# A gated delta rule stage with its units reordered, small transposes and sums taken off the matrix engine, and its steps placed anew

## What is computed

```python
qkv = causal_conv_silu(concat([d_q, d_k, d_v]), conv_w)
q = l2norm(q) * DN_HEAD_DIM ** -0.5 ; k = l2norm(k)
g = -exp(dn_a_log) * softplus(d_a + dn_dt_bias) ; beta = sigmoid(d_b)
# per chunk of C tokens, per head
decay = exp(where(tri, g_cum_i - g_cum_j, -inf))
a = where(strict, (k * beta) @ k.T * decay, 0)
T = inverse(a + eye)                         # unit lower triangular
value = T @ (v * beta) ; k_cumdecay = T @ (k * beta * exp(g_cum))
attn_intra = where(tri, q @ k.T * decay, 0)
# over the chunks, with the state S
v_new = value - k_cumdecay @ S
o = (q * exp(g_cum)) @ S + attn_intra @ v_new
S = S * exp(g_last) + (k * exp(g_last - g_cum)).T @ v_new
out_b = rmsnorm(o) * silu(d_z)
```

## Time and profile before

| | us |
|---|---|
| median of 3 runs (lowest, highest) | 2085.27 (2084.6, 2088.63) |
| the profiled execution | 2087.39 |
| its span, first to last instruction | 2085.8 |
| PE busy | 2041.2 (98%) |
| DVE busy | 1043.2 (50%) |
| ACT busy | 840.2 (40%) |
| POOL busy | 140.3 (7%) |

### The profile page before, as it was taken

One profiled execution on the slowest core, in us unless ns is written; L12 is line 12 of the kernel. 1 busy time (PEld: TensorE's weight loads), 2 busy tenths in 40 slices (PEclk: granted clock), 3 DMA queues, 4 the chain that ended last, 5 costly groups with the idle time before them and its releaser, 6 DMA issues.

```text
span 2085.8 us, 28890 instructions
## 1 busy us (share of the span) xinstructions
PE 2041.2 (98%) x9864; PEld 1677.5 (80%) x9864; DVE 1043.2 (50%) x1773; ACT 840.2 (40%) x1612; POOL 140.3 (7%) x162
## 2 busy tenths in 40 slices
PE   7999999999999999999999999999999999998999
PEld 6788778887888888878878888888888888887887
DVE  5644564656566555464454444454444444445332
ACT  6643344443443434443344434343343444344221
POOL 1000010211121111001100000000000000000110
PEclk9999999999999999999999999999999999999999
DMA  9422111111111121224432222222212222222432
GB/s 369 185 101 80 61 62 60 66 55 59 62 60 60 40 80 61 91 96 137 150 131 87 78 88 85 80 85 80 105 73 94 80 85 80 94 73 100 151 134 77
DMA packets 31858, 198.10 MB, mean 95 GB/s; under 512 B 4016, under 2 KB 4144, under 8 KB 11088
## 3 DMA queue, kind: packets, MB, share of 16 engines
q1 hardware_dynamic: 23040, 164.64, 22.0%
q0 software_dynamic: 8064, 30.81, 4.1%
q10 hardware_dynamic: 720, 2.19, 0.3%
HBM read 189.23 MB, written 8.39 MB: 95 GB/s over the span
## 4 chain that ended last, share of the span: by engine, by line
PE 85%; DVE 8%; ACT 3%; issue 2%; DMA 2%; DVEq 0%; ACTq 0%; POOL 0%; SPq 0%
PE gemm L1119 71%; PE pb L1119 11%; DVE w_lo L636 2%; PE pb L1122 2%; DMA raw<-in_w 1%; DVE scratch L815 1%; DMA scratch<-in_memT 1%; ACT scratch L315 1%; ACT w_hi L303 0%; DVE scratch L893 0%; DVE scratch L911 0%; DVE scratch L816 0%; DMA scratch<-in_rows_in 0%; ACT scratch L342 0%; DVE scratch L806 0%
## 5 line engine op out<-in xcount | busy, mean ns | idle before, releaser
L1119 PE MATMUL gemm<-act_lo,w_hi 128*128 128x512 f32 x2512 | 978.3, 392 | 13.8 <-DVE act_lo L657 11.3
L1119 PE MATMUL gemm<-act_hi,w_hi 128*128 128x512 f32 x2384 | 965.4, 405 | 10.0 <-DVE act_lo L645 9.8
L1119 PE MATMUL gemm<-act_hi,w_lo 128*128 128x512 f32 x2384 | 933.4, 392 | 0.0
L1119 PEld LDWEIGHTS gemm<-act_lo,w_hi 128*128 128x128 f32 x2512 | 475.1, 189 | 111.1 <-issue 20.4
L1119 PEld LDWEIGHTS gemm<-act_hi,w_hi 128*128 128x128 f32 x2384 | 450.0, 189 | 103.0 <-issue 17.6
L1119 PEld LDWEIGHTS gemm<-act_hi,w_lo 128*128 128x128 f32 x2384 | 448.8, 188 | 97.3
L636 DVE TENSOR_TENSOR w_lo<-raw,w_hi 128x512 fp32r<-128x512 f32 x624 | 398.9, 702 | 251.1 <-ACT w_hi L303 249.2
L303 ACT ACTIVATE w_hi<-raw 128x512 fp32r<-128x512 f32 x624 | 341.2, 618 | 402.1 <-PE gemm L1119 388.9
L1119 PEld LDWEIGHTS pb<-scratch 128*128 128x128 f32 (+1 forms) x1440 | 190.4, 188 | 44.4 <-issue 17.2
L1119 PE MATMUL pb<-scratch 128*128 128x64 f32 (+6 forms) x1440 | 218.5, 292 | 0.9 <-DVE scratch L928 0.2
L240 POOL TENSOR_TENSOR scratch<-scratch,cst 128x512 f32<-128x512 f32 x56 | 78.3, 1404 | 483.7 <-DVE scratch L890 290.9
(11 more groups left out here) (202 smaller groups left out, 1331.9 us busy)
## 6 DMA issues: line engine op xcount, KB each, us to landing
raw<-in_w SPq DMA_DIRECT2D x156, 1024.0 KB, 4.8
scratch<-in_rows_in POOLq DMA_DIRECT2D x6, 1024.0 KB, 6.4
big<-in_xT POOLq DMA_DIRECT2D x4, 1024.0 KB, 13.0
scratch<-in_xT POOLq DMA_DIRECT2D x16, 256.0 KB, 3.1
x<-big POOLq DMA_DIRECT2D x16, 256.0 KB, 2.3
scratch<-x POOLq DMA_DIRECT2D x16, 256.0 KB, 4.0
outT<-scratch POOLq DMA_DIRECT2D x16, 256.0 KB, 3.8
scratch<-in_memT ACTq DMA_DIRECT2D x4, 512.0 KB, 9.7
```

The source lines that it names most:

```text
L1119: return nc.tensor.matmul(out, a, b, start=start, stop=stop, skip_group_check=skip)
```

## The change

- **Units.** The order of a head's units is q, k, z, v (the weights are laid out so). The z unit's gate goes to a tile ZN of its own and is copied to SZ when the head before is out.
- **Gate rows by DMA.** `gate_rows` on PE and `sel` on POOL go. DVE transposes the gate columns once, POOL's queue writes them to DRAM (`rows_dram`), and for each head two DMAs read them back to all partitions (GROW, BROW), issued between POOL's masks of level 1 and 2 of the head before.
- **Transposes.** Level 0's and those of levels 2 to 5 go from PE to DVE (`V.transpose`, blocks of 32x32), level 6's stays.
- **Sums.** The norm sums and the output sum are two float32r matmuls, on a square that ACT writes twice (rounded, whole) and DVE's difference of the two.
- **Recurrence.** `negated_keys` goes. `kept_keys` multiplies the scaled keys with the state, DVE subtracts that from VB (VD), and `new_values` is one matmul on VD.
- **Placement.** `products` of head h stands in unit v of head h itself; levels 1 and 2 of a head beside the next head's q, 3 and 4 beside k, 5 and 6 beside z, the recurrence beside v. On DVE the convolution comes ahead of `lo`, and `lo` is split into quarters between the steps of the recurrence.
- **Start.** The memory's loads are issued by POOL's queue; each quarter of x follows when the same quarter of the memory is there.

The diff, cut to its core:

```diff
+            def rows(h):
+                for j, row in enumerate((GROW, BROW)):
+                    pool.dma_start(row.rearrange("p (c t) -> p c t", t=P), rows_dram[j].rearrange("(c h) t -> h c t", h=DN)[h].partition_broadcast(P))\
+                        .then_inc(sem["rows_in"], 16)
...
+            for q in range(4):
+                c = slice(4 * q * MEM, 4 * (q + 1) * MEM)
+                pool.dma_start(MEMRAW[:, c], memT[:, c]).then_inc(sem[f"tile_in{q}"], 16)
             for q in range(4):
+                pool.wait_ge(sem[f"tile_in{q}"], 16)
...
+                    if k == 1 and not last:
+
+                        pool.wait_ge(sem["kb"], h + 1)
+                        pool.wait_ge(sem["eg"], h + 1)
+                        pool.wait_ge(sem["dec_in"], h + 1)
+                        rows(h + 1)
...
+            def squares(hi_part, whole, src, done):
+
+                A(hi_part, src, ACT.Square)
+                A(whole, src, ACT.Square).then_inc(sem[done], 1)
...
+            def q_or_k(h, j, p=None):
+                conv(h, j, j)
+                if p is not None:
+                    level(p, 3 + 2 * j)
+                dn_lo(h, j, (0, 1))
                 dve.wait_ge(sem["dn_sig"], 4 * h + j + 1)
                 V.tensor_tensor(SS, Y, E, ALU.mult).then_inc(sem["dn_s"], 1)
+                dn_lo(h, j, (2, 3))
+                dve.wait_ge(sem["dn_sq"], 2 * h + j + 1)
+                V.tensor_tensor(NSL, SQ, NSH.bitcast(F32), ALU.subtract).then_inc(sem["dn_sl"], 1)
+                if p is not None:
+                    level(p, 4 + 2 * j)
+                    [values_and_keys, keys_of_state][j](p)
+                if j == 1:
+                    decay(h, p is None)
...
+                V.tensor_tensor(KB, KTT, BROW, ALU.mult).then_inc(sem["kb"], 1)
+                if p is None:
+                    dn_lo(h, 2)
+                else:
+                    recurrence(p, lambda q: dn_lo(h, 2, (q,)))
+                dve.wait_ge(sem["dec_e"], h + 1)
+                st.then(V.tensor_tensor(v3(DEC), v3(DEC), chunks(C["tri_from"]), ALU.mult))
+                dve.wait_ge(sem["kk"], 2 * h + 1)
+                V.tensor_tensor(AT, pb[2][:, :], DEC, ALU.mult).then_inc(sem["at"], 1)
+                dve.wait_ge(sem["dn_sig"], 4 * h + 3)
+                st.then(V.tensor_tensor(ZN, Y, E, ALU.mult))
...
+                    out_low(p)
+                    dve.wait_ge(sem["vn_ps"], NB * h)
                 level(h, 0)
...
+                    V.tensor_tensor(v3(YI), chunks(C["ident"]), v3(blk(ML, 0, NB)), ALU.subtract).then_inc(sem["yt"], 1)
+                    dve.wait_ge(sem["yt"], (LEVELS - 2) * h + 1)
+                    V.transpose(XI, YI).then_inc(sem["xy"], 1)
...
+                    if k < LEVELS - 2:
+                        dve.wait_ge(sem["xy"], n)
+                        V.transpose(YI, XI).then_inc(sem["yt"], 1)
...
-                mm(pb[0][:, :], C["ones"], SQ).then_inc(sem["dn_ss"], 1)
+                mm(pb[0][:, :], sums[:, P:2 * P], NSH, True, False)
+                mm(pb[0][:, :], sums[:, P:2 * P], NSL, False, True).then_inc(sem["dn_ss"], 1)
...
+            def kept_keys(h, c):
+
+                pe.wait_ge(sem["st"], (NB - 1) * h + c)
+                mm(pb[3][:, P:2 * P], blk(KGT, c), ST).then_inc(sem["ks_ps"], 1)
...
+                part(0, 0, 2)
                 level_u(p, 1)
+                part(0, 2, 5)
                 level_w(p, 1)
+                part(0, 5, 9)
+                level_u(p, 2)
+                part(0, 9, 13)
+                level_w(p, 2)
+                part(0, 13, KT)
+                for j in (1, 2):
                     part(j, 0, 1)
+                    level_u(p, 2 * j + 1)
                     part(j, 1, 4)
+                    level_w(p, 2 * j + 1)
+                    if j == 1:
+                        part(1, 4, 6)
+                        transposes(p)
+                        part(1, 6, 9)
+                    else:
+                        part(2, 4, 9)
+                    level_u(p, 2 * j + 2)
                     part(j, 9, 12)
+                    level_w(p, 2 * j + 2)
+                    part(j, 12, 14)
                     if h is not None:
                         norm_sum(h, j - 1)
+                    part(j, 14, KT)
+                new_values(p, 0)
                 part(3, 0, 1)
+                chunk_out(p, 0)
+                part(3, 1, 2)
+                for c in range(1, NB):
+                    part(3, 3 * c - 1, 3 * c)
+                    kept_keys(p, c)
+                    part(3, 3 * c, 3 * c + 1)
                     new_values(p, c)
+                    part(3, 3 * c + 1, 3 * c + 2)
                     chunk_out(p, c)
+                    if c == 1 and h is not None:
+                        products(h)
+                part(3, 11, 15)
                 out_sum(p)
                 part(3, 15, KT)
```

More of the change, by code:

```diff
@@ L226, in _, with head @@
                 pool.wait_ge(sem["row_sq"], t - 1)
-                pool.dma_start(ROWS[t % 2], rows_in[t]).then_inc(sem[f"row_in{t % 2}"], 16)
-            pool.wait_ge(sem["ab_fin"], 1)
-            pool.wait_ge(sem["sp_done"], GM)
-            sel(0)
-            def levels(h):
+                pool.dma_start(ROWS[t % 2], rows_in[t]).then_inc(sem[f"slot_in{t % 2}"], 16)
+            pool.wait_ge(sem["rows_t"], 2)
+            for j in range(2):
+                for q in range(NB):
+                    t = slice(q * 32, (q + 1) * 32)
+                    pool.dma_start(rows_dram[j][:, t], gate_rows[t, j * 32:(j + 1) * 32]).then_inc(sem["rows_out"], 16)
+            pool.wait_ge(sem["rows_out"], 16 * 2 * NB)
+            pool.wait_ge(sem["mixed"], XA)
+            rows(0)
+            def head(h, last=False):
                 pool.wait_ge(sem["at"], h + 1)
@@ new lines, in z_of_head, with v_of_head @@
+            def z_of_head(h, p=None):
+                if p is not None:
+                    new_value(p, 0)
+                dn_hi(h, 2)
+                if p is not None:
+                    new_value(p, 1)
+                tables(h, p is None)
+                if p is not None:
+                    new_value(p, 2)
+                sigmoid("dn_y", 4 * h + 3, "dn_sig")
+                if p is not None:
+                    new_value(p, 3)
+                    out_norm(p)
+            def v_of_head(h):
+                level(h, 1)
+                dn_hi(h, 3)
+                sigmoid("dn_y", 4 * h + 4, "dn_sig")
+                level(h, 2)
@@ L717, in _ @@
             dve.wait_ge(sem["ab_e"], 1)
-            V.tensor_tensor(gate["ebg"][:, :], gate["ebg"][:, :], gate["beta"][:, :], ALU.mult).then_inc(sem["ab_fin"], 1)
+            for j, name in enumerate(("gc", "beta")):
+                V.transpose(gate_rows[:, j * 32:(j + 1) * 32], gate[name][:, :]).then_inc(sem["rows_t"], 1)
             def gelu(u, slot, n, dst, mid=None):
@@ L1355, in out_sum @@
             def out_sum(h):
-                pe.wait_ge(sem["o_sq"], h + 1)
-                mm(pb[0][:, :], C["ones"], OSQ).then_inc(sem["o_ss"], 1)
+                pe.wait_ge(sem["o_sl"], h + 1)
+                mm(pb[0][:, :], sums[:, P:2 * P], OSH, True, False)
+                mm(pb[0][:, :], sums[:, P:2 * P], OSL, False, True).then_inc(sem["o_ss"], 1)
             def beside(part, p, h=None):
-                part(0, 0, 4)
-                products(p)
-                part(0, 4, 7)
-                transposes(p)
```

428 lines of the change are left out of this document (188 added, 240 removed).

## The result

The changed kernel takes 2026.75 us (2026.17 to 2028.26) beside 2085.64 us (2084.6 to 2088.63) for the kernel before: a ratio of 0.9716, interval 0.97 to 0.9733. Its profiled execution took 2026.43 us with a span of 2024.6, so the span fell by 61.2 where 49.1 was forecast. The direction came out as forecast, and so did most parts of the change in kind; the split of new_values, forecast as a cost, was none. The gain is a quarter larger than the sum said, and the time lies just under the low end of the range (2027).

The account below looks back on a forecast made before the run. PE, busy 98% of the span, was taken to bound the kernel. 2087.4 - 43.9 (work leaving PE) - 8.3 - 2.1 (waits that go) + 2.4 + 2.8 (waits that come) = 2038.3, as a median 2036 us, range 2029 to 2044 (wider range 2027 to 2060).

Parts of the forecast that it names:

- the split of new_values: Recurrence on PE: groups of four records become two groups of two for new_values 1 to 3, costing +0.42 us a head.
- There is a fixed part of some 0.13 in each group: Recurrence on PE: each small group between gemm matmuls costs some 0.13 us besides its records.
- Level 0's transposes: Level 0 on PE: four transposes leave PE for DVE, saving 0.43 us a head.
- level 2's wait: PE's wait for DVE ahead of level 2's transposes goes: 1.1 us a loop turn, 8.3 us in all.
- the square's 2.1 us: Head 0's norm sums: PE's two waits for ACT's square go, 2.1 us together.
- The last head: Last head's recurrence: kept_keys(1) waits 2.0 us and ACT's sigmoid costs 0.4; with small ones +2.8 us.
- The start: Kernel start: memory loads on POOL's queue with x behind them, up to 2 us either way, taken as 0.
- B: Rival: level 0 and DVE's order cost more, slow DVE transposes or masks add 8 to 20 us, say 2050; chance 0.27.
- D: Rival: DVE becomes the chain, its turn 77 us a head, the kernel slower at 2133; chance 0.05.
- E: Rival: a wait for each us that left PE, the period stays 71 us, 2081 to 2089; chance 0.04.
- C: Rival: everything falls into place, no new waits and mem's loads free of x's, 2029; chance 0.08.
- The step from 2038.3 to 2036: Whole kernel: from profiled execution to median, since the three timed runs' median lay 2.1 us below that execution.

Follow-up runs that it names:

- b_products_later: The kernel before with products one part (k step) later in its gemm unit: 2087.17 us against 2087.16, ratio 0.9999.
- a_all_places_moved: Changed kernel with diagonal group four parts later, memory loads on ACT's queue, second norm sum earlier, kept_keys(2), kept_keys(3) and out_sum moved: 2020.2 us, ratio 0.9676.
- b_values_later: The kernel before with two parts instead of one between a chunk_out and the next new_values, negated_keys earlier, out_sum later: 2094.24 us, ratio 1.0031.
- a_diag_later: The changed kernel with the one-time group that waits for the diagonal matrices four parts later in its gemm unit: 2021.74 us, ratio 0.9689.

## Why the prediction was off

- **The reading of what bounds it** held: PE at 98%, each us off its stream a us off the kernel.
- **The step that failed is "There is a fixed part of some 0.13 in each group".** It was read off, where groups of the recurrence stand in front of data waits of 0.1 to 0.2 us. Two records cost 0.23, four 0.46, six 0.70. The prediction's own prices leave both readings open: its 0.94 for eight records and 0.71 for six are 0.118 a record, and only the groups of two and four stand above that. What decides is a group where nobody waits, and the kernel before has such groups in its last head, chunk_out(0) and new_values(1) with four records each (timeline of PE):

```profile
844.62 0.60 PE L1119 MATMUL pb<-scratch 128*128 128x128 f32 x4
...
845.75 0.60 PE L1119 MATMUL pb<-scratch 128*128 128x128 f32 x4
...
846.89 0.83 PE L1119 MATMUL pb<-scratch 128*128 128x128 f32 x6
```

  845.75 - 844.62 - 0.68 = 0.45 and 846.89 - 845.75 - 0.68 = 0.46, against 0.68 and 0.57 in the loop. So the split of new_values costs 0 and not +0.42; and the waits behind the false price were there to be gained. All recurrence groups with products: before 6.62 a head, after 6.29, -0.33, where the prediction had +0.29 and +0.1 for kept_keys(1). That is 0.7 of the 1.26 us a head by which the period of 65.1 was missed.
- **Level 0's transposes**: 0.66 gone, not 0.43. Their price is 0.43 to 0.47, the rest was another hidden wait. The levels together, level 2's wait included, gave 2.94 for 2.72, where 2.72 has in it a new wait of 0.1 at level_u(1) that didn't come. negated_keys gave 1.06 for 1.0, the key and value transposes 0.07. Against these stand 0.09 for the three pairs of sums, priced at 0.45 and measured at 0.48 (0.59 for the output sum, with its forecast wait of 0.1 in it). Together they make up the other 0.5.
- **What was right**: the norm sums (0.88 to 0.48, held by their experiment), gate_rows (1.34 gone), four transposes at 0.43 to 0.45 (held by theirs), the square's 2.1 us, 40 records fewer, DVE's 48 us, the transpose's 0.71 for 0.69, out_sum's 0.11. By the estimate from the Trainium skill, "VectorE: DVE Perf Modes", section "The three transpose paths" (four times 311 ns, 1.24 us), the kernel would have been 4 to 5 us slower than forecast; the row decides against it, with 0.71.
- **The last head** gave 6.6 for 3.1. The wait of kept_keys(1) lengthened chunk_out(0)'s group to 1.86 from a free 0.46, so 1.4 in place of the 2.0 for it (783.41 - 780.19 - 1.36 = 1.86), and no 0.4 for the sigmoid showed. Its recurrence, too, had no split cost to pay, and two groups of it had held waits in the kernel before: chunk_out(1) cost 1.05 and chunk_out(3) 0.80 there, 0.69 and 0.46 now.
- **The start** cost 1.1 for 0 in this pair of profiles: the wait for L372 met a lower granted clock behind it. That isn't shown to be the change's doing. The kernel before has the same wait (L361, 1.9 us) with 1.00 behind it, and b_products_later, whose start is the same as that kernel's, waits 2.8 us and then has 0.66. Head 0 starts at 233.3 to 236.7 us in the seven profiles with the changed kernel's start, at 233.9 to 236.3 in the four with the old one. The prediction named a range of 2 either way, for another reason, the loads.
- **Rivals.** B (2050) fell with the transposes' duration. D (2133) fell: DVE worked 48 of 63.8 us and held PE up in the last head only, beside the hidden waits of some 0.5 us a head that a_all_places_moved took out. E (each us that left replaced by a wait) is refuted by the period. C, "everything falls into place" (2029), was nearest, and still too careful, since it kept the false prices. The low end of the range, 2027, was set by C alone; that the split costs nothing if the 0.13 is waiting was open to be asked, as a bound from below, and was not.
- **The step from 2038.3 to 2036** went the right way by luck: it took the first three executions of the kernel before, whose median lay 2.1 under the profiled one, for typical, and 16 later ones have a median of 2087.16. Against the sum itself the miss is 11.5 us, not 9.

In sum the span fell 12.1 us more than forecast: 8.4 in the loop (1.2 a turn by the unit starts, 1.26 by the ledger of one turn), 3.5 in the last head, 0.2 in head 0 and 1.1 behind the stage, less 1.1 at the start. The stage itself (8.4, 3.5 and 0.2) is thus the whole of it, and what lies outside cancels. The 1.1 behind the stage are mostly the granted clock where the first projection starts: the same stretch in the kernel before, then in the changed kernel (windows view):

```profile
900.00:910.00 10.00, 6.17 (x14) 4.46 (x15) 8.87 (x15) 9.01 (x17) 0.00 (x0) 0.66 0.01 2
```

```profile
840.00:850.00 10.00, 5.82 (x18) 4.24 (x19) 8.94 (x15) 9.15 (x17) 0.00 (x0) 0.83 0.00 0
```

The unit there is 0.8 us shorter at 0.83 than at 0.66. No experiment looked into it.

## What to carry to other kernels

Price a small group between pipelined matmuls from the places where nobody waits (the first or last turn of a loop, with the producers long done), and compare it with the same group inside the loop; what is more inside is a wait that no view lists, and moving the step by a part gives it back. Before a step is given more room, look what stands on the other side of it: of the experiments on the kernel before, b_values_later lost more at its neighbours than it won, and b_products_later only moved a wait on. And a part of a change that loses alone, as the split sums did, can pay once the order around it gives its producer time. What a profile shows outside the stage that was changed, the start above all, has to be held against other profiles of the same code before it is called a cost.

## What the runs showed of the hardware

- A plain fp32 matmul of 128x128 costs 0.115 to 0.117 us per record beside gemm matmuls in groups of 2, 4 and 6 (0.23, 0.46, 0.70), and 0.113 in larger ones (1.80 for 16, 2.48 for 22, 2.72 for 24). So a fixed part of a group, if there is one, is about 0.01 us by these prices and not 0.13.
- DVE's transpose of a 128x512 fp32 tile took 0.71 us (40 of them), as long as an operation on two such tiles takes with no mask beside it (0.69, L830); a plain copy of one (L887) took 0.43.
- Two loads on POOL's queue, issued 0.8 us apart for the other heads, were 5.6 us apart once in the changed kernel's trace (a gap of 4.8) and once with a third load (4.8 again), where a gap of 7.1 stood ahead of the third load of another head; nothing in the trace says why.
- The granted clock at the change of layers was not the same in kernels that differ only earlier. PE worked 6.34 of the 10 us ahead of it in both of these, the changed kernel first (1.00 in those 10 us) and a_diag_later second (0.96), and then was granted:

```profile
1025.00:1032.00 7.00, 6.38 (x15) 3.95 (x14) 7.00 (x12) 7.00 (x13) 0.00 (x0) 0.51 0.41 150
```

```profile
1022.00:1029.00 7.00, 7.00 (x24) 4.53 (x23) 7.00 (x11) 7.00 (x13) 0.00 (x0) 0.81 0.39 150
```

  The unit there took 13.3 and 11.3 us. So 2 us of the difference between these two kernels lies here, far behind the edit, and isn't the price of any instruction that it moved. Whether an edit decides which way the clock falls isn't shown.
